# Two chunks later for the transposed rows in the expert loop, and the fold behind the first down chunk

## The reference

```
h = rmsnorm(x) * (1 + scale_f) + shift_f
logits = h @ w_router + b_router ;  top 4 of 32 experts per token, softmax weights
for each expert e, over its rows xb:
    gu   = xb @ w_e1[e] + b_e1[e]              # w_e1[e]: 1024 x 2048, float32
    gate = min(gu[:, :1024], 7) ; up = clip(gu[:, 1024:], -7, 7)
    act  = (up + 1) * (gate * sigmoid(1.702 * gate))
    y    = act @ w_e2[e] + b_e2[e]             # w_e2[e]: 1024 x 1024, float32
x = x + gate_f * rmsnorm(sum over the token's 4 experts of weight * y)
```

## Time and profile before

| What | Number |
|---|---|
| runs of the kernel before, median (lowest to highest) | 2012.2 us (2007.26 to 2012.99) |
| the profiled execution, span inside it | 2007.64 us, 2005.9 us |
| PE busy | 1649.6 us, 82% |
| DVE busy | 1553.1 us, 77% |
| ACT busy | 1175.7 us, 59% |
| DMA over the span | 519.83 MB, mean 259 GB/s |
| `lo` of an expert chunk (line 1554) | 388 x 2285 ns |
| `hi` of an expert chunk (line 971) | 388 x 1907 ns |
| loads of expert chunks | 396 of 1 MB, which are 33 blocks of 12 |
| granted TensorE clock, mean | 0.931 |

### The profile page before, as it was taken

How to read it: one execution, slowest core, us unless ns; L and a number is a source line. 1 busy time by engine, 2 the same in 40 slices (tenths; PEclk the granted TensorE clock), 3 DMA queues, 4 the chain that set the end, 5 groups by cost and what they waited for, 6 DMA issues and landing times.

```text
span 2005.9 us, 21977 instructions
## 1 busy us (share of the span) xinstructions
PE 1649.6 (82%) x7163; PEld 1287.9 (64%) x7163; DVE 1553.1 (77%) x1306; ACT 1175.7 (59%) x1078; POOL 251.7 (13%) x282
## 2 busy tenths in 40 slices
PE   2899999988985578888889889889889889889742
PEld 2667677866775467667767767767767767767531
DVE  5788656565536789899899899899899899898746
ACT  1256721656214176776776776776776776776631
POOL 0300001000000111211211211211211211210110
PEclk8899999999995699999999999999999999999865
DMA  7433145211164289998998998898898898898435
GB/s 294 124 134 130 66 160 176 85 42 64 63 220 187 90 325 347 357 367 338 356 364 337 350 362 337 346 362 336 350 355 339 343 355 337 344 354 334 196 130 211
DMA packets 112512, 519.83 MB, mean 259 GB/s; under 512 B 16210, under 2 KB 49330, under 8 KB 58162
## 3 DMA queue, kind: packets, MB, share of 16 engines
q1 hardware_dynamic: 98970, 491.34, 64.5%
q0 software_dynamic: 8224, 17.23, 2.4%
q10 hardware_dynamic: 5272, 10.67, 1.4%
HBM read 509.48 MB, written 19.14 MB: 264 GB/s over the span
## 4 chain that ended last, share of the span: by engine, by line
PE 45%; DVE 28%; issue 12%; ACT 11%; DMA 3%; DVEq 0%; POOL 0%; ACTq 0%; POOLq 0%
PE ps L1959 15%; DVE lo L1554 15%; PE ps L1701 9%; PE ps L1969 7%; ACT hi L971 5%; PE ps L1886 2%; PE ps L1901 2%; PE ps L1956 2%; DVE gmin L1584 2%; PE ps L1948 1%; DVE gmin L1579 1%; DVE act_h L1577 1%; ACT hi L757 1%; PE ps L1940 1%; DMA xt<-x_dram 1%
## 5 line engine op out<-in xcount | busy, mean ns | idle before, releaser
L1554 DVE TENSOR_TENSOR lo<-raw,hi 128x2048 fp32r<-128x2048 f32 x388 | 869.2, 2285 | 78.0 <-ACT hi L971 77.8
L971 ACT ACTIVATE hi<-raw 128x2048 fp32r<-128x2048 f32 x388 | 719.5, 1907 | 101.9 <-PE ps L1969 95.4
L1959 PE MATMUL ps<-hi,xT 128*128 128x512 f32 x1568 | 430.0, 403 | 17.4 <-DVE lo L1554 17.3
L1969 PE MATMUL ps<-hi,aT 128*128 128x512 f32 x784 | 246.9, 414 | 123.4 <-DVE lo L1554 123.4
L1959 PEld LDWEIGHTS ps<-hi,xT 128*128 128x128 f32 x1568 | 289.8, 190 | 91.0 <-DVE lo L1554 32.3
L1959 PE MATMUL ps<-lo,xT 128*128 128x512 f32 x1056 | 284.3, 391 | 0.0
L1969 PEld LDWEIGHTS ps<-hi,aT 128*128 128x128 f32 x784 | 148.5, 196 | 179.1 <-DVE lo L1554 148.2
L1701 PE MATMUL ps<-hT,hi 128*128 128x512 f32 x720 | 240.9, 410 | 15.5 <-DVE lo L1143 8.5
L1959 PEld LDWEIGHTS ps<-lo,xT 128*128 128x128 f32 x1056 | 199.3, 189 | 43.2
L648 POOL TENSOR_TENSOR ticks<-eps 128x1 f32<-128x1 f32 x100 | 79.0, 790 | 852.2 <-ACT ysb L1005 810.2
L1969 PE MATMUL ps<-lo,aT 128*128 128x512 f32 x528 | 178.3, 421 | 0.0
(11 more groups left out here) (308 smaller groups left out, 1946.4 us busy)
## 6 DMA issues: line engine op xcount, KB each, us to landing
raw<-w_e_dram SPq DMA_DIRECT2D x396, 1024.0 KB, 6.4
raw<-w_ada_dram SPq DMA_DIRECT2D x24, 1024.0 KB, 7.5
raw<-w_in_dram SPq DMA_DIRECT2D x15, 1024.0 KB, 5.6
raw<-w_merge_gate_dram SPq DMA_DIRECT2D x8, 1024.0 KB, 5.3
yk<-yk_d SPq DMA_DIRECT2D x4, 2048.0 KB, 14.6
raw<-w_branch_rnn_dram SPq DMA_DIRECT2D x8, 640.0 KB, 4.5
raw<-w_branch_attn_dram SPq DMA_DIRECT2D x4, 1024.0 KB, 5.0
raw<-w_out_dram SPq DMA_DIRECT2D x4, 1024.0 KB, 4.8
```

The source lines that it names most:

```text
L971: s.activation(hi[i % HS][:, :], raw[i][:, :], ACT.Copy).then_inc(hi_done, 1)
L1554: v.tensor_tensor(lo[i][:, :], raw[i][:, :], hi[i % HS][:, :].bitcast(F32), ALU.subtract).then_inc(split_done, 1)
L1959: last = mm(ps[:, q, :], x_[:, i, xa:xa + P], w[:, q * 512:(q + 1) * 512], start=False, stop=i == M1 - 1, skip_group_check=True)
L1969: last = mm(ps[:, 4 + h, :], aT[:, k, xa:xa + P] if cap == CAP_A else aT[:, k, 0:P], w[:, kk * DE + h * 512:kk * DE + (h + 1) * 512], star ...
```

## The change

Lists are changed on three engines; nothing is added or removed.

- ACT and DVE take the turned activations (`hi_a`, `lo_a`) after chunk 5 instead of chunk 3 (`iteration_a`, and ACT's list for extra blocks) or chunk 4 (`iteration_b`, which is also DVE's list for extra blocks).
- They take the turned tokens (`hi_x`, `lo_x`) later as well: in `iteration_a` after chunk 8 instead of 6, in `iteration_b` after chunk 9 instead of 7. `late` blocks keep theirs.
- In `iteration_a` ACT's `y_copy` moves from before chunk 4 to after chunk 7; in `iteration_b` from after chunk 6 to after chunk 7. `select` of DVE's `iteration_b` stays behind chunk 8.
- PE's `fold_up` in `iteration_b` follows down chunk 8 instead of down chunk 9. PE's other orders stay.

```diff
 # ACT
             def iteration_a(b):
-                hi_ws(b, 0, 4)
+                hi_ws(b, 0, 6)
                 hi_a(b, CAP_B)
+                hi_ws(b, 6, 8)
                 act.wait_ge(chunk_used, b(MS, UP0))
                 y_copy(b, 2, CAP_A)
-                hi_ws(b, 4, 7)
+                hi_w(b, 8)
                 hi_x(b, CAP_B)
-                hi_ws(b, 7, 11)
+                hi_ws(b, 9, 11)
                 up_complete(b)
                 sigmoid(b, CAP_A)
                 hi_w(b, 11)
...
 # ACT, iteration_b
                     y_low()
-                hi_w(b, 4)
+                hi_ws(b, 4, 6)
                 hi_a(b, CAP_A)
-                hi_ws(b, 5, 7)
+                hi_ws(b, 6, 8)
                 if y:
                     act.wait_ge(ylow_used, nb(1, -1))
                     y_copy(b, 2, CAP_B)
-                hi_w(b, 7)
+                hi_ws(b, 8, 10)
                 if not more_b:
                     hi_x(b, CAP_A)
-                hi_ws(b, 8, 11)
+                hi_w(b, 10)
                 up_complete(b)
                 up_low()
...
 # ACT, iteration_over
-                hi_ws(b, 0, 4)
+                hi_ws(b, 0, 6)
                 hi_a(b, CAP_B)
-                hi_ws(b, 4, 11)
+                hi_ws(b, 6, 11)
...
 # DVE
             def iteration_a(b):
-                lo_ws(b, 0, 4)
+                lo_ws(b, 0, 6)
                 lo_a(b, CAP_B)
-                lo_ws(b, 4, 7)
+                lo_ws(b, 6, 9)
                 lo_x(b, CAP_B)
-                lo_ws(b, 7, 9)
                 select(b, CAP_B)
                 lo_w(b, 9)
...
             def iteration_b(b, nb, before, after, late=False):
-                lo_ws(b, 0, 5)
+                lo_ws(b, 0, 6)
                 lo_a(b, before)
-                lo_ws(b, 5, 8)
+                lo_ws(b, 6, 9)
+                select(b, after)
+                lo_w(b, 9)
                 if not late:
                     lo_x(b, after)
-                lo_w(b, 8)
-                select(b, after)
-                lo_ws(b, 9, 11)
+                lo_w(b, 10)
...
 # PE, iteration_b
                     down_chunk(i, CAP_B if over else CAP_A)
-                    if i == M1 + 1:
+                    if i == M1:
                         fold_up(nb)
```

## The result

The changed kernel takes 1924.76 us (median of 4 runs, 1924.34 to 1925.58) against 2009.73 us (median of 4) for the kernel before beside it: a ratio of 0.9579, with 95% interval 0.9557 to 0.9600. Forecast were 1928 us, and a sum of 1924.8 before the allowance for the median. The span of the profiled execution is 1923.8 us, 82.1 less.

What follows compares the result with a forecast made beforehand. Bound: a ring of three engines in step, DVE nearest to full. Gains: 14 pairs x 5.3 = 74, -1, 2.7 block ahead, 1.6 + 3.5 pair behind, 2 extra block: 83 us, giving 1924.8; plus 3 for the median, 1928 us; range 1912 to 1962.

Steps and rivals of the forecast that it cites:

- the walk: Hand timing of ACT, DVE and PE through one pair of iterations: 5.3 us less, 75.1 to 69.8.
- iteration_b, 3.7 us: In iteration_b DVE never waits before lo 5 to 7, and glu_clip starts at 1115.4 instead of 1119.14.
- iteration_a, 1.6 us: In iteration_a PE never waits in the up part, and glu_clip starts at 1153.05 instead of 1154.69.
- One sign of the list: DVE has one wait in a pair, about 3.4 us before glu_clip of iteration_a, released by L1959.
- some 1.1 us of that: In iteration_b, the part of the 3.7 us that comes from the fold's place behind down chunk 8.
- The clock, taken at 0 after the change: PE's slow stretch comes again at the head of iteration_b at no cost; bounds 0 and 1.7 us a pair.
- The first rival: A slow clock stretch on PE's path in every pair takes 1.7 us back: 1954 us, chance 0.18.
- DMA, no cost: Loads at 377 GB/s on average for a 69.8 us pair were taken to cost nothing.
- its buffer is wanted only one iteration on: In iteration_a POOL's scatter starts 7 us later with y_copy, but its buffer is free again within 8 us.
- The extra block, 2 us,: The extra block's 3.45 us wait before chunk 4 shrinks: gain between 0 and 3.5 us, taken as 2.
- The third rival: Late up_low makes the fold hold PE, with down chunks 9 to 11 behind it: 2017 us, chance 0.03.
- The fourth: Moving hi_a frees nothing since PE held hi 4 and 5; only the fold counts: 1991 us, chance 0.04.

Runs made afterwards that it cites:

- Experiment 9: The changed kernel with lo_x of iteration_b done twice, one more DVE instruction of 1.15 us into spare memory: 1936.99 us, ratio 0.9636.
- experiment 6: The changed kernel with glu_out of iteration_b moved behind lo 0 of the next iteration_a on DVE: 1903.36 us, ratio 0.9471.
- 8: The changed kernel with lo_x of iteration_a done three times, two more DVE instructions of 0.65 us into spare memory: 1924.14 us, ratio 0.9578.
- experiment 2: The changed kernel with fold_up put back behind down chunk 9: 1944.08 us, ratio 0.9673.
- experiment 1: The kernel before with only fold_up moved behind down chunk 8: 1967.28 us, ratio 0.9791.
- experiment 3: The kernel before with only ACT's and DVE's iteration_a lists as in the change: 1975.39 us, ratio 0.9839.
- experiment 5: The changed kernel with POOL's gather ahead of its scatter in iteration_b: 1922.24 us, ratio 0.9565.

## Why the prediction was right

The size came out, and so did the mechanism: waits of DVE that the old orders caused are gone, and each half of a pair is shorter by what the walk gives. Two steps beside it failed, POOL's and the extra block's, and nearly cancelled.

- *iteration_b, 3.7 us.* B fell from 39.57 to 35.69, 3.9. Shifted to the pair shown above (20.2 us earlier), the walk has `lo_a` at 1081.67 (measured 1081.67), the fold at 1093.3 (1093.00, after a wait of 0.33) and the clip at 1095.2 (1095.08). Experiment 9 shows that DVE is the bound there.
- *iteration_a, 1.6 us.* A fell from 35.51 to 33.93. From the bias at 1104.26 the walk has the clip at 1129.0; measured 1129.00. Experiments 6 and 8 show that PE is its bound, and DVE isn't. One sign of the list wasn't met: DVE's remaining waits don't stand before `glu_clip` in one piece of 3.4 us. In the pair shown only 1.20 do; 2.1 stand before four `lo`, each for a `hi` that waits for PE. The walk itself had `hi` 9 and 10 held by PE, so the sentence contradicted it.
- *The fold, "some 1.1 us of that".* As the last step it is 1.1 to 1.4 us (experiment 2). As the only one it is 2.4 a pair (experiment 1). The share of a part that overlaps with another depends on which is taken first; the prediction gave one figure as if it were the part's own.
- *The clock, taken at 0 after the change.* PE's time at the slow clock costs nothing in the new `iteration_b`, as I said. I had the shift of 1.1 us between the first pair and the others in the rows, but read it as a risk for later. It was a cost before: 1.2 us of the 3.9 in `iteration_b` are a slow stretch that the new order hides. Nor did it "come again" in every pair, but in 7 of 13, and the other 6 are those that lost time through POOL. The first rival, 1.7 us a pair, didn't come about; no run had a whole slow stretch inside the up part of `iteration_a`, so its price there isn't shown. (Once in experiment 2 it reached about 0.2 us into it, and A was 34.05 instead of 33.93.)
- *DMA, no cost.* Right to 383 GB/s at a share of 0.97 (experiment 6). By the Trainium skill's 358 GB/s (DMA: Bandwidth & Descriptors, "Where 436 GB/s comes from") neither the changed kernel (372 GB/s over 920 us) nor that of experiment 6 could have been that fast. The runs decide against it as a limit for this core running alone.
- *POOL: "its buffer is wanted only one iteration on".* This step failed. I moved POOL's start and left its durations as they were. In the changed kernel they are longer beside DVE's rows without a gap (an issue of 15.12 us), tokens come late in 6 pairs, and 6.7 us are lost.
- *The extra block, 2 us,* was too small: its B fell from 41.84 to 37.26, 4.6. That the sum was right to 1 us is in part luck: three errors met, 7 us lost to POOL, 3 gained in this block, and 3 gained by 0.2 us more in each `iteration_b`. The 3 us added for the median have no ground in the runs either: the changed kernel's median lies 0.8 us below its profiled execution. Rivals 3 and 4 were priced without this allowance.
- *The third rival,* PE held by the fold, is the 0.33 us above (2.3 us in all from 860 to 1780 us) and no more. *The fourth,* that moving `hi_a` frees nothing, falls with experiment 3, where nothing but `iteration_a`'s lists is moved and A is 1.6 us shorter in every pair.

## What to carry to other kernels

When engines run fixed lists in step, look for an engine that waits in front of one instruction while the next one in its list could run, as ACT did for 7.13 us before `hi_a`; moving that instruction back can be priced by hand, from start to start, to a few tenths. Price each part alone and as the last one, since their gains overlap. And when the busiest engine loses its gaps, look at what another engine did in them.

## What the runs showed of the hardware

POOL's small operations and its DMA issues wait while DVE works through a row of `tensor_tensor` with both inputs in SBUF: 8.37 us for an addition that takes 0.19, 15.12 us for the issue of a gather that takes 1. The addition ends at 1021.03, and the last `lo` of DVE's row at 1020.98. The issue ends 0.94 us after the next instruction behind the row starts. In the kernel before, the addition that started at 1112.83 ended at 1117.00, and DVE's row at 1116.95, with the 2.2 us gap before `glu_clip` of `iteration_b` behind it.

```profile
1112.46 4.49 DVE L1554 TENSOR_TENSOR lo<-raw,hi 128x2048 fp32r<-128x2048 f32 x2
```

```profile
1112.83 4.17 POOL L648 TENSOR_TENSOR ticks<-eps 128x1 f32<-128x1 f32 x1 [1.94 <-DMA yk_d<-ysb,idx_now]
```

The Trainium skill (SBUF — State Buffer, "SBUF: two separate sides") says that GpSimd and VectorE share a pair of SBUF ports, that a VectorE instruction with two SBUF inputs takes it exclusively against a GpSimd operation that reads SBUF, and that the other then blocks. The traces agree, with one thing more: between the instructions of a row without gaps POOL often wasn't let in either, through six of them in the case of 15.12 us. That the ports are the cause is by that page. The runs show the coincidence in time, at these places and in experiment 5, and that with another row of DVE the same issue takes 3.20 us (experiment 9).
